# A two-layer hybrid encoder step: the combined projection and the RWKV scan rebuilt

## What is computed

```
x = x + 0.5 * swiglu(rmsnorm(x, n1), f1g, f1u, f1d)
z = rmsnorm(x, nm) @ w_in_l                  # one combined projection, 3944 columns
# its columns feed three groups of heads:
#   fox:       8 heads of attention with forget gates (the sample tokens also see 512 cached ones)
#   RWKV-7:    4 heads, decays w, gates a and g from low-rank products of the projected columns
#   retention: 4 heads, chunkwise, with rotary embedding
x = x + concat([o_fox, o_rwkv, o_ret]) @ w_out_l
x = x + 0.5 * swiglu(rmsnorm(x, n2), f2g, f2u, f2d)
x = x + sigmoid(x @ w_pg) * rmsnorm(pe @ w_pp, pn)
```

```
Skk = einsum('bhvk,bhk->bhv', S, kk_t)
S = S * w_t - Skk (kk_t * a_t)^T + v_t k_t^T
o_t = einsum('bhvk,bhk->bhv', S, r_t)
```

## Time and profile before

| | us |
|---|---|
| median of 3 runs | 1617.86 (1614.76 to 1618.06) |
| the profiled execution | 1610.07 |
| its span in the trace | 1608.5 |
| PE busy | 1518.1 |
| VectorE busy | 854.8 |
| ScalarE busy | 592.2 |
| GpSimd busy | 193.3 |

### The profile page before, as it was taken

The page is one execution under the profiler, slowest core; times in us unless marked ns, Lnnn a source line. Parts: engine busy times, 40 slices in busy tenths (PEclk is TensorE's granted clock), DMA queues, the critical chain, the costliest instruction groups (busy, mean ns, idle before and its releaser), DMA issues. The chain is left out here.

```text
span 1608.5 us, 27103 instructions
## 1 busy us (share of the span) xinstructions
PE 1518.1 (94%) x11140; PEld 1427.1 (89%) x11140; DVE 854.8 (53%) x1238; ACT 592.2 (37%) x871; POOL 193.3 (12%) x127
## 2 busy tenths in 40 slices
PE   7999999978998999999989999998899989999997
PEld 6999989978776899999979999898787678999997
DVE  4555344787526455553555553447783353555535
ACT  4433333432114444333443442344310244434324
POOL 0000016741011000000000000175500200000000
PEclk9999999989657999999989999999895679999999
DMA  7444433421011245444334444343300122444443
GB/s 297 168 156 162 177 126 118 152 106 57 7 35 57 106 157 181 158 169 171 136 136 158 167 172 157 105 157 131 134 2 11 60 79 106 153 160 173 168 161 134
DMA packets 32017, 209.77 MB, mean 130 GB/s; under 512 B 4384, under 2 KB 6064, under 8 KB 7744
## 3 DMA queue, kind: packets, MB, share of 16 engines
q1 hardware_dynamic: 29376, 200.38, 34.2%
q0 software_dynamic: 2560, 8.26, 1.4%
HBM read 204.53 MB, written 4.10 MB: 130 GB/s over the span
## 5 line engine op out<-in xcount | busy, mean ns | idle before, releaser
L810 DVE TENSOR_TENSOR split_w<-wc,split_w 128x2048 fp32r<-128x2048 f32 x140 | 320.5, 2292 | 370.3 <-ACT split_w L521 370.3
L521 ACT ACTIVATE split_w<-wc 128x2048 fp32r<-128x2048 f32 x140 | 268.4, 1917 | 532.4 <-PE bank L1291 334.2
L1285 PE MATMUL bank<-split_x,split_w 128*128 128x288 f32 x2816 | 393.2, 296 | 14.5 <-ACT split_x L527 14.5
L1285 PEld LDWEIGHTS bank<-split_x,split_w 128*128 128x128 f32 x2816 | 380.4, 189 | 19.2 <-ACT split_w L521 12.3
L1308 PE MATMUL bank<-split_x,split_w 128*128 (+1 forms) x2112 | 282.3, 295 | 0.0
L1308 PEld LDWEIGHTS bank<-split_x,split_w 128*128 128x128 f32 x2112 | 281.9, 188 | 0.0
L1291 PE MATMUL bank<-split_x,split_w 128*128 128x288 f32 x1408 | 199.9, 294 | 0.0
L1291 PEld LDWEIGHTS bank<-split_x,split_w 128*128 128x128 f32 x1408 | 190.2, 188 | 0.3
L421 POOL TENSOR_TENSOR split_x<-wc,split_x 128x1024 fp32r<-128x1024 f32 x32 | 78.4, 2451 | 506.9 <-ACT split_x L565 506.9
L565 ACT ACTIVATE split_x<-wc 128x1024 fp32r<-128x1024 f32 x62 | 65.4, 1058 | 114.1 <-PE bank L1362 114.1
L1359 PE MATMUL bank<-split_h,split_x 128*128 128x288 f32 x496 | 84.8, 312 | 7.6 <-ACT split_h L570 7.4
(11 more groups left out here) (291 smaller groups left out, 1700.2 us busy)
## 6 DMA issues: line engine op xcount, KB each, us to landing
wc<-wcol SPq DMA_DIRECT2D x174, 1024.0 KB, 4.7
wc<-wfirst SPq DMA_DIRECT2D x12, 1024.0 KB, 4.9
con<-consts_in SPq DMA_DIRECT2D x1, 2294.0 KB, 16.8
arena<-kc_in POOLq DMA_DIRECT2D x8, 256.0 KB, 3.0
arena<-vc_in POOLq DMA_DIRECT2D x2, 1024.0 KB, 5.1
xT<-x_in SPq DMA_DIRECT2D x2, 576.0 KB, 4.3
k_out<-zT POOLq DMA_DIRECT2D x8, 144.0 KB, 2.2
v_out<-zT POOLq DMA_DIRECT2D x8, 144.0 KB, 2.4
```

What stands on the lines that cost most here:

```text
L521: act.activation(ws[s % 2][0], wc[:, p % RING, :], ACT.Copy).then_inc(S["cast"], 1)
L810: dve.tensor_tensor(lo, wc[:, (POS_FFN[f] + s) % RING, :], hi, ALU.subtract).then_inc(S["wlo"], 1)
L1285: pe.matmul(o, hi[:, k, cs], x[:, k, :], start=(w == 0 and k == 0), stop=False)
```

## The change

It touches the projection's preparation, the masks, and everything from `atok` to the outputs.

- **Low parts.** GpSimd's 31 subtractions go; VectorE has `z_rest(n)` in its own list, between the steps of the RWKV preparation. Loops of the projection on ScalarE and GpSimd are written out.
- **No reciprocals.** A sigmoid's 1/(1+e) becomes a logarithm and an exponential on ScalarE (`inverse_of_one_plus`), for the small input, the four low-rank products, the retention gate and the attention gate (`fg`, now between ScalarE's copies of the levels). The constant of the decay goes into the scale of the exponentials.
- **Places.** PE's small products come earlier: the low-rank products after block 10 (17 before), the head sums after block 12 (19), the first rotations after block 17 (23), the bonus after block 18 (23), the last rotations after block 23 (29).
- **Masks.** Products of the two head halves alternate, and VectorE's masks follow that order.
- **Scan.** Instead of `atT`, `atok` is kept by token. For all nine chunks at once PE makes a 64x64 transition product per head (36 products) and the chunk's own state input (72 products). The step of a chunk is then: state = transition x state (PE, four products) plus a prepared term, to which VectorE has added the decayed state (L1092's kind); one addition ends it. Chunks 8 (the sample) and 0 share the first step. The outputs split into a part without the state (`out_within`), made beside the steps, and one with it (`out_across`), whose reading vectors are corrected once (`read_with`). Retention's outputs alternate the head halves, and both halves lie in one bank.

```diff
-                    def rest(n, i=0):
-                        hi, lo = zw[n % 2]
-                        pool.wait_ge(S["zcast"], i * 8 + n + 1)
-                        pool.tensor_tensor(lo, z_raw(n), hi, ALU.subtract).then_inc(S["zlo"], 1)
...
+                    def inverse_of_one_plus(e, ready):
+                        link(act.activation(e, e, ACT.Ln, bias=col(C_ONE)))
+                        act.activation(e, e, ACT.Exp, scale=-1.0).then_inc(S[ready], 1)
+                    for n in range(9):
+                        z_block(n)
+                    act.wait_ge(S["small"], 1)
+                    link(act.activation(esm, zT[:, Z_SMALL, :], ACT.Exp, scale=col(C_SMALLSC)))
+                    inverse_of_one_plus(esm, "e_small")
...
-                    def sigmoid_of(e):
-                        link(dve.tensor_scalar(e, e, 1.0, None, ALU.add))
-                        link(dve.reciprocal(e, e))
+                    def z_rest(n):
+                        hi, lo = zw[n % 2]
+                        dve.wait_ge(S["zcast"], n + 1)
+                        dve.tensor_tensor(lo, z_raw(n), hi, ALU.subtract).then_inc(S["zlo"], 1)
...
+                    order = [(j, b, e) for j in range(3) for b in range(2) for e in range(2)]
+                    for j, b, e in order:
+                        hs, g = slice(64 * e, 64 * e + 64), 2 * e + b
+                        for q in range(TILES[j][1] // CH):
+                            rows, at = slice(CH * q, CH * q + CH), 128 * j + HD * b
+                            mm = pe.matmul(bank[4 + q][hs, at:at + HD], atok[rows, j, HD * g:HD * g + HD],
+                                           tok[rows, j, 2 + b, hs], start=True, stop=True)
+                    mm.then_inc(S["mh_ps"], 1)
...
+                    with_step = {0: [(read_with, 0), (read_with, 1), (read_with, 2)], 1: [(out_within, 1)],
+                                 2: [(out_within, 0)], 3: [(ret_tok, 0), (ret_scores, 0)],
+                                 4: [(out_within, 2), (ret_tok, 1)], 5: [(ret_scores, 1), (ret_tok, 2)],
+                                 6: [(ret_scores, 2), (out_across, 0)],
+                                 7: [(ret_kv, 0), (ret_kv, 1), (ret_kv, 2), (ret_kv, 3), (ret_kv, 4)]}
+                    done = 0
+                    pe.wait_ge(S["hc"], 4)
+                    for step, chunks in enumerate(SCAN):
+                        pe.wait_ge(S["mtc"], min(step + 1, 4))
+                        if step:
+                            pe.wait_ge(S["s_ok"], done)
+                        for at_, i in enumerate(chunks):
+                            j, q = chunk(i)
+                            done += 1
+                            for b in range(2):
+                                for e in range(2):
+                                    hs, m = slice(64 * e, 64 * e + 64), MT_AT[q] + 128 * j + HD * b
+                                    mm = pe.matmul(bank[(step + at_) % 2][hs, HD * b:HD * b + HD], mt[hs, m:m + HD],
+                                                   st[hs, i if i < 8 else 9, b, :], start=True, stop=True)
                             mm.then_inc(S["s_ps"], 1)
```

The order of VectorE's list in the projection, with the low parts between the steps:

```diff
+                    z_rest(14)
+                    for b in range(2):
+                        dve.wait_ge(S["kk_ps"], b + 1)
+                        dve.tensor_scalar(khat[:, b, :], bank[4 + b][:, 0:T], 1e-24, None, ALU.max).then_inc(S["kln"], 1)
                     dve.tensor_tensor(eexc, lc, lw, ALU.subtract).then_inc(S["dexc"], 1)
...
+                    z_rest(15)
                     dve.wait_ge(S["rn"], 2)
                     link(dve.tensor_tensor(kkf, kkf, khat, ALU.mult))
+                    z_rest(16)
...
+                    z_rest(17)
+                    dve.wait_ge(S["small"], N_SHIFTED)
```

More of the change, by code:

```diff
@@ L292, in pa, with chunk @@
             return par[rows, a:a + 1]
+        def chunk(i):
+            return (i // 4, i % 4) if i < 8 else (2, 0)
         def mats_psum(j, e):
@@ new lines, in _ @@
+                    done = 0
+                    dve.wait_ge(S["mh_ps"], 2)
+                    for q in range(4):
+                        w = 384 if q == 0 else 256
+                        dve.tensor_copy(kv[:, MT_AT[q]:MT_AT[q] + w], bank[q][:, 0:w]).then_inc(S["hc"], 1)
+                    for step, chunks in enumerate(SCAN):
+                        dve.wait_ge(S["hc"], min(step + 1, 4))
+                        for i in chunks:
+                            j, q = chunk(i)
+                            old, at = i if i < 8 else 9, MT_AT[q] + 128 * j
+                            end = CH * (i + 1) - 1
+                            if 0 < i < 8:
+                                dve.wait_ge(S["s_ok"], i + 1)
+                            for b in range(2):
+                                h = kv[:, at + HD * b:at + HD * b + HD]
+                                chained(dve.scalar_tensor_tensor(h, st[:, old, b, :], einc[:, b, end:end + 1], h,
+                                                                 ALU.mult, ALU.add))
+                        for at_, i in enumerate(chunks):
+                            j, q = chunk(i)
+                            new, at = i + 1 if i < 8 else 10, MT_AT[q] + 128 * j
+                            done += 1
+                            dve.wait_ge(S["vchain"], n_chain[0])
+                            dve.wait_ge(S["s_ps"], done)
+                            ms = bank[(step + at_) % 2][:, 0:128].rearrange("p (b n) -> p b n", b=2)
+                            dve.tensor_tensor(st[:, new, :, :], ms, kv[:, at:at + 128].rearrange("p (b n) -> p b n", b=2),
+                                              ALU.add).then_inc(S["s_ok"], 1)
+                        for also, which in with_step.get(step, ()):
+                            also(which)
@@ new lines, in _ @@
+                    for j, b, e in order:
+                        hs, g = slice(64 * e, 64 * e + 64), 2 * e + b
+                        at = 128 * j + HD * b
+                        for q in range(TILES[j][1] // CH):
+                            rows = slice(CH * q, CH * q + CH)
+                            pe.matmul(bank[q][hs, at:at + HD], tok[rows, j, 4 + b, hs], tok[rows, j, 6 + b, hs],
+                                      start=True, stop=False)
+                        for q in range(TILES[j][1] // CH):
+                            rows = slice(CH * q, CH * q + CH)
+                            mm = pe.matmul(bank[q][hs, at:at + HD], tok[rows, j, 2 + b, hs],
+                                           u0[rows, j, HD * g:HD * g + HD], start=False, stop=True)
@@ L1554, in _, with out_within @@
-                        pe.wait_ge(S["u_ok"], 2 * i + 2)
+                                g = 2 * e + b
+                                mm = pe.matmul(bank[4 + j][64 * e:64 * e + 64, n * b:n * b + n],
+                                               atok[0:n, j, HD * g:HD * g + HD], ctm[0:n, j, 128 * g:128 * g + n],
+                                               start=True, stop=True)
+                        mm.then_inc(S["rp_ps"], 1)
+                    def out_within(j):
+                        n = TILES[j][1]
+                        if j == 2:
+                            pe.wait_ge(S["owc"], 2)
@@ new lines, in _ @@
+                    pe.wait_ge(S["hc"], 4)
+                    for step, chunks in enumerate(SCAN):
+                        pe.wait_ge(S["mtc"], min(step + 1, 4))
+                        if step:
+                            pe.wait_ge(S["s_ok"], done)
+                        for at_, i in enumerate(chunks):
+                            j, q = chunk(i)
+                            done += 1
+                            for b in range(2):
+                                for e in range(2):
+                                    hs, m = slice(64 * e, 64 * e + 64), MT_AT[q] + 128 * j + HD * b
+                                    mm = pe.matmul(bank[(step + at_) % 2][hs, HD * b:HD * b + HD], mt[hs, m:m + HD],
+                                                   st[hs, i if i < 8 else 9, b, :], start=True, stop=True)
+                            mm.then_inc(S["s_ps"], 1)
+                        for also, which in with_step.get(step, ()):
+                            also(which)
@@ L1587, in _ @@
[L1587 to L1603 removed]
+                        nch = 2 if j < 2 else 1
```

465 lines of the change are left out of this document (239 added, 226 removed).

## The result

The changed kernel took 1524.69 us (median of 4 runs, 1523.82 to 1528.41) beside 1617.36 us for the kernel before: a ratio of 0.9434, interval 0.9415 to 0.9453. The gain of 92.7 us is larger than the 69.9 us forecast. The profiled execution took 1523.82 us with a span of 1522.3 us.

A forecast was written before the change was run, and what follows sets the result against it. PE bounds the kernel, so only its idle, low-clock or removable work can be won. 1.5 + 15.6 - 0.7 + 18.5 = 34.9 us a layer, 69.8 in all: 1540.3 us profiled, times 1.0048 gives 1548 us; range 1522 to 1578.

The forecast's parts named there:

- What bounds the kernel: Whole kernel: PE is busy 94% of the span; only its idle, low-clock or removable time can be won.
- Start, 1.5 us: Start of the projection: PE starts 1.5 us earlier a layer without GpSimd's first two low parts; from 0 to 3.
- Projection, 15.6 us: Block 6's end to block 30's: 82.4 instead of 98.0 us if PE never waits; gain 15.6 a layer, down to 5.
- The cover: Projection: VectorE and ScalarE, in order, finish before PE asks; closest is block 17's cast, ready at 34.7, wanted at 35.1.
- Masks, -0.7 us: Masks and levels: 0.4 us gained by masks without gaps, 1.1 lost on `atok`; -0.7 a layer, from -2.5 to 0.
- Scan and outputs, 18.5 us: Scan to outputs: 38.5 instead of 57.0 us, busiest tile's passes at low clock; gain 18.5 a layer, from 5 to 27.
- the clock stays up: Rival, scan: dense 32-row products could keep 2.4 GHz; about 8 us a layer, 1532 us; chance 0.13.
- The factor 1.0048: Final sum: the runs' median is 1.0048 times the profiled execution, turning 1540.3 into 1548 us.
- The signs: Projection without PE waits over a microsecond, 82 us; scan about 38 us, steps 2 to 4 apart; other stages' clock steady.
- One bank for two row halves: Rival, chunk products, `out_across`, retention states: row tiles of one bank take turns; 11.5 us a layer back, 1571 us; chance 0.14.
- VectorE late: Rival, projection: VectorE's chains come late as a whole; 13 of the 15.6 us are lost, 1574 us; chance 0.12.
- Draining between 32-row tiles: Rival, transition and input products: 216 passes cost a lone pass each, 67 us instead of 4.5; 1673 us; chance 0.04.

The follow-up runs named there:

- rest_pool: The changed kernel with the projection's 31 low parts back on GpSimd, everything else as changed; 1540.9 us in a single run.
- early: The changed kernel with the first level of tile 0 moved into PE's wait for the masks; 1523.73 us, ratio 0.9415.
- scan_only: The kernel before with the new masks, scan, outputs and the forget gate's inverse on ScalarE, its projection unchanged; 1562.42 us, ratio 0.9664.
- turns: The changed kernel with transition products, input products and `out_across` sorted so that one tile's passes follow each other; 1560.46 us in a single run.
- fill: The changed kernel with 36 useless 128x128 products in PE's wait for VectorE's masks; 1526.47 us, ratio 0.9450.
- fill_all: The changed kernel with four mask copies on ScalarE, 10 useless products in the mask wait and 7 ahead of the first chunk; 1520.31 us, ratio 0.9409.
- after_again: The changed kernel unchanged, run again as yardstick on the chip of other kernels; 1525.55 us, ratio 0.9458.

## Why the prediction was right, point by point

The time lies near the lower end of the range (1522 to 1578), 23 us below the forecast. That it is inside rests on the clock's case being in the range, not on the sum: what the sum priced at half clock ran in large part at the full one. The excess, 21 us by stages, is 18 in the scan and 5 in the attention, less 2 in the rest.

**What bounds the kernel** held: both parts of the gain lie where PE idled or ran at half clock.

**Start, 1.5 us**: measured 1.5 in both layers, and `rest_pool` loses just that.

**Projection, 15.6 us**: 83.3 instead of 82.4 us, a gain of 14.5 between the same starts. The cover held: PE waits for no low part, not even at the cast of block 17 with its 0.4 us. The missing 0.9 us lies behind the small products, which cost what was charged: the next eight passes take 1.17 to 1.27 us to the following start instead of 1.07, five times (286.88 to 288.15 is one), and the sum had nothing for that. The view that VectorE's order decides is borne out by `rest_pool`: its stretched instructions bring back 4.2 us of waits.

**Masks, -0.7 us**: -1.1 and -1.0. `atok` cost 0.7 instead of 1.1. What the step left out: PE's products for the masks end 3 us sooner, VectorE's masks only 0.5, so PE idles 6.4 us instead of 3.7 and then runs 0.8 to 0.9 us longer up to `atok`, at half clock at first.

**Scan and outputs, 18.5 us**: 26.0 and 29.0; the second is above the term's own range of 5 to 27. The step that was mis-sized is the clock that all its terms were charged at. Term by term, layer 0, from the starts in PE's timeline:

| term | charged | measured |
|---|---|---|
| transition and input products | 4.5 | 4.5, of which 1.4 idle |
| VectorE's copies | 1.5 | 1.6 |
| `read_with` | 2.7 | 2.5 |
| nine chunk products | 4.5 | 3.8 |
| `out_within` | 5.5 | 3.9 |
| retention transposes, scores, key-value | 7.6 | 4.4 |
| `out_across` | 4.5 | 2.3 |
| retention outputs | 5.2 | 5.6 |
| two waits for VectorE | 2.5 | 2.6 |

Stretches of `read_with` and of the retention outputs, PE alone:

```profile
406.95:409.43 2.48, 2.48 (x27) 0.50 0.00 0
425.59:431.14 5.55, 5.55 (x64) 0.61 0.06 24
```

`read_with`, at half clock, came out 0.2 us below its charge; `out_across`, at full clock, took half. The retention outputs took 0.4 us more than charged although a part of them ran at the full clock, so that term was counted low. That the transition and input products took just the 4.5 us charged is luck: 3.2 us of work at the full clock and 1.4 us of idle time. Counting the passes of the busiest tile was right for `read_with` and `out_across`; 0.50 for all of it was not. The rival "the clock stays up", 8 us a layer and 0.13, is what mostly happened. The charge of 38.5 us at half clock was itself low beside the 43 us that the line gives as an estimate.

**Attention, not in the sum**: 3.6 and 1.8 us. The instructions of this stretch are almost the same; its clock is 0.77 and 0.78 instead of 0.75. With the new scan ahead of it the stretch takes 39.8 (`early`, layer 1, at 0.91) to 47.9 us (`scan_only`, layer 0, at 0.75), so this gain is not a fixed part of the change.

**The factor 1.0048** did not carry over: the changed kernel's profiled run was 0.9 us from the median of its runs. The stages' 91.3 us and the 92.7 of the medians agree within the spread of the runs.

**The signs** given: no wait on VectorE between blocks and 83 us held; "about 38 us" for the scan did not (31.2 and 28.3), and its steps start 1.6 to 3.3 us apart instead of 2 to 4. The other stages' clock moved by the attention's 3.6 us, which the prediction had named as a sign of being wrong if it was more than a few.

**Rivals.** One bank for two row halves: refuted for `out_across` (`turns`). The Trainium skill, TensorEngine Tiling (Array Packing), Restrictions and Gotchas, bars different row tiles from one PSUM bank at the same time; here the measurement decides: disjoint partition halves were written at once. VectorE late: refuted, as above. Draining between 32-row tiles: refuted, 216 passes in 4.5 us, a fifteenth of the 67 us of that case. For the cost of a change of tile shape, the row at 413.97 shows eight paired passes taking 0.38 us to the next shape's start where four steps of 0.052 to 0.0675 (the 32-column passes of `turns` and of the changed kernel) would make 0.21 to 0.27: an estimate of 0.11 to 0.17 us a change, somewhat below the 0.19 of the prediction. These passes have 64 columns, so it is rough.

**Open:** why the clock of one and the same scan differs from layer to layer. In the levels idling was shown to cost it (`fill`); in the scan no run controlled it, and `fill_all`'s attempt didn't.

## What to carry to other kernels

Price a rebuilt stage at both clock levels and give both sums: here the sum at one level alone missed the stage by 7 to 10 us a layer. Count short products by the busiest tile of the array, and issue them so that neighbours in the queue use different tiles. Keep GpSimd's arithmetic out of a stretch in which PE waits for VectorE's chains (one run showed it here); and take a gain in one stage as won only once the clock of the next ones is read.

## What the runs showed of the hardware that was not expected

- The granted clock follows more than PE's busy share: `early` is busy 36.55 of 37.1 us at 0.79, `fill` 32.05 of 32.5 at 1.00, with the same kind of products.
- After some 200 short passes that start within 2.6 us, PE stands 1.37 us with nothing that the profile shows to wait for (403.95, "issue"; 1.55 in layer 1, 0.7 in `after_again`); sorted by tile, and so slower, the same products show no such gap. That the instructions came too slowly was not tried.
- A feed-forward stretch of 1056 passes has two durations. PE alone, the changed kernel's two layers, then the same stretch of layer 0 before:

```profile
519.70:663.40 143.70, 143.63 (x1056) 0.99 0.44 157
1273.60:1412.40 138.80, 138.74 (x1057) 1.00 0.45 161
```

```profile
564.80:703.60 138.80, 138.71 (x1056) 1.00 0.44 161
```

The clock's 0.01 explains about 1.4 us (143.7 x 0.01) of the 4.9; the passes are otherwise 134.8 ns apart instead of 131.4. The two rates change between layers and executions of one kernel: 827 and 848 passes start in 110 us of it in the changed kernel's two layers, 827 in both of `after_again`, 848 and 849 in those of `fill_all`. No edit of this case touches it, and it can pass for a gain.
